# Causal masks of the second score pass: added by VectorE in PSUM instead of by a TensorE product, in a decoder trunk of two layers

## The reference

```python
def causal_block_attention(q, k, v, log_decay_cum=None):
    scale = q.shape[-1] ** -0.5
    for blk in range(T // Q_BLOCK):
        lo, hi = blk * Q_BLOCK, (blk + 1) * Q_BLOCK
        s = jnp.einsum('bqhd,bkhd->bhqk', q[:, lo:hi], k[:, :hi]) * scale
        ...
        mask = (lo + jnp.arange(Q_BLOCK))[:, None] >= jnp.arange(hi)[None, :]
        p = jax.nn.softmax(jnp.where(mask, s, -jnp.inf), axis=-1)
        outs.append(jnp.einsum('bhqk,bkhd->bqhd', p, v[:, :hi]))
```

## Time and profile before

| | |
|---|---|
| median of 3 runs | 2460.87 us (2460.1 to 2465.82) |
| span of the profiled execution | 2455.2 us |
| the six attentions together, in the span | 682.9 us |
| PE / DVE / ACT / POOL busy | 93% / 48% / 36% / 37% |

### The profile page before, as it was taken

The page is one execution under the profiler, slowest core; times in us unless marked ns, Lnnn a source line. Parts: engine busy times, 40 slices in busy tenths (PEclk is TensorE's granted clock), DMA queues, the critical chain, the costliest instruction groups (busy, mean ns, idle before and its releaser), DMA issues.

```text
span 2455.2 us, 35075 instructions
## 1 busy us (share of the span) xinstructions
PE 2293.2 (93%) x14164; PEld 1750.4 (71%) x14164; DVE 1172.6 (48%) x2262; ACT 876.3 (36%) x1444; POOL 902.2 (37%) x962
## 2 busy tenths in 40 slices
PE   7988999999999999879999889999999999998898
PEld 7866878986695876545697678789857859664456
DVE  4278243525336127666333881446162452277662
ACT  4332124714334334333333222156143244333341
POOL 2255112215525410555422642122345263115552
PEclk9989999999999999989999999999999999999899
DMA  4100232230100113100321003312301002131003
GB/s 151 56 19 1 87 107 87 70 137 1 35 18 1 50 56 120 60 1 1 138 70 56 19 2 98 121 61 95 112 1 35 18 1 69 37 137 43 1 1 129
DMA packets 92016, 141.28 MB, mean 58 GB/s; under 512 B 18352, under 2 KB 65488, under 8 KB 91856
## 3 DMA queue, kind: packets, MB, share of 16 engines
q1 hardware_dynamic: 91856, 139.05, 16.6%
HBM read 105.48 MB, written 33.55 MB: 57 GB/s over the span
## 4 chain that ended last, share of the span: by engine, by line
PE 79%; DVE 14%; ACT 2%; issue 2%; POOL 2%; DMA 0%; SPq 0%; POOLq 0%; DVEq 0%; ACTq 0%
PE psum L240 37%; PE psum L504 12%; PE psum L1392 5%; PE psum L1354 3%; DVE gla_A L766 3%; PE psum L1375 3%; PE psum L1340 3%; PE psum L1378 3%; PE psum L1380 3%; PE psum L745 2%; PE psum L1399 1%; PE psum L997 1%; POOL w_lo L198 1%; PE psum L1778 1%; PE psum L882 1%
## 5 line engine op out<-in xcount | busy, mean ns | idle before, releaser
L198 POOL TENSOR_TENSOR w_lo<-w_raw,w_hi 128x512 fp32r<-128x512 f32 (+3 forms) x240 | 322.1, 1374 | 823.6 <-ACT w_hi L189 823.6
L240 PE MATMUL psum<-h_hi,w_hi 128*128 128x512 f32 x768 | 200.8, 404 | 0.0
L240 PE MATMUL psum<-h_lo,w_hi 128*128 128x512 f32 x768 | 199.1, 403 | 0.0
L1587 POOL TENSOR_TENSOR mla_acc<-mla_acc,mla_p 128x512 f32<-128x512 f32 (+3 forms) x160 | 159.7, 1015 | 103.1 <-ACT mla_p L1446 103.1
L240 PE MATMUL psum<-h_hi,w_lo 128*128 128x512 f32 x768 | 192.2, 392 | 0.0
L240 PE MATMUL psum<-w_hi,h_hi 128*128 128x256 f32 (+3 forms) x1280 | 183.7, 286 | 0.0
L240 PE MATMUL psum<-w_hi,h_lo 128*128 128x256 f32 (+3 forms) x1280 | 179.6, 283 | 0.0
L240 PE MATMUL psum<-w_lo,h_hi 128*128 128x256 f32 (+3 forms) x1280 | 179.4, 283 | 0.0
L1587 POOL TENSOR_TENSOR fox_acc<-fox_acc,fox_p 128x512 f32<-128x512 f32 (+3 forms) x160 | 149.9, 958 | 75.5 <-ACT fox_p L1446 75.4
L189 ACT ACTIVATE w_hi<-w_raw 128x2048 fp32r<-128x2048 f32 (+3 forms) x60 | 113.6, 1893 | 175.1 <-PE psum L504 169.8
L240 PEld LDWEIGHTS psum<-h_lo,w_hi 128*128 128x128 f32 x768 | 147.7, 195 | 32.1
(11 more groups left out here) (324 smaller groups left out, 4428.8 us busy)
## 6 DMA issues: line engine op xcount, KB each, us to landing
w_raw<-in_w_in_dram SPq DMA_DIRECT2D x38, 1024.0 KB, 5.3
out_dram<-x_rows SPq DMA_DIRECT2D x64, 512.0 KB, 2.7
x_rows<-out_dram SPq DMA_DIRECT2D x56, 512.0 KB, 5.2
w_raw<-in_w_out_dram SPq DMA_DIRECT2D x16, 1024.0 KB, 6.5
x_first<-in_x_dram SPq DMA_DIRECT2D x8, 512.0 KB, 7.0
x_rows<-in_x_dram SPq DMA_DIRECT2D x8, 512.0 KB, 6.0
w_raw<-in_w_in_dram SPq DMA_DIRECT2D x2, 1088.0 KB, 8.7
w_raw<-in_w_in_dram SPq DMA_DIRECT2D x2, 1056.0 KB, 5.2
```

Source lines behind the costliest of these rows:

```text
L198: last = pool.tensor_tensor(self.w_lo[c["set"]][:, at], self.w_raw[c["set"]][:, at], self.w_hi[c["set"]][:, at].bitcast(F32), ALU.subtract)
L240: last = pe.matmul(o, lhs, rhs, start=(kk == 0 and n == 0), stop=(kk == KT - 1 and n == 2))
L1587: pool.tensor_tensor(acc, acc, p, ALU.add).then_inc(self.acc_done.sem, 1)
```

## The change

The product L1382 is gone. In its place VectorE adds a table `key_mask` (the mask with keys down the partitions, 128x128 in bf16) to the 128 queries in the bank, in place, after the third product of the unit (`mask`, waits for `st_done`). It is the first thing that VectorE does in unit j of `vector`. The exponents of diagonal units wait for that addition (`st_masked`) and no longer for TensorE. The identity in bf16, which only L1382 used, gives its place to the new table. The first pass is as it was.

```diff
@@ scores_turned
-        diagonal = kb >= 4 * c
-        last = pe.matmul(out, self.k_lo[ks][:, a, keys], self.q_hi[qs][:, a, lo:], start=False, stop=not diagonal)
-        if diagonal:
-            last = pe.matmul(k.psum[:, u % 2, lo:lo + P], k.mask_bf[:, :], k.ident_bf[:, :], start=False, stop=True)
-        last.then_inc(self.st_done.sem, 1)
+        pe.matmul(out, self.k_lo[ks][:, a, keys], self.q_hi[qs][:, a, lo:], start=False, stop=True)\
+          .then_inc(self.st_done.sem, 1)
@@ exponent
-        act.wait_ge(self.st_done.sem, self.st_done.at(u + 1))
+        if self.diagonal(i, j):
+            act.wait_ge(self.st_masked.sem, self.st_masked.at(self.masks(i, j) + 1))
+        else:
+            act.wait_ge(self.st_done.sem, self.st_done.at(u + 1))
@@ new
+    def mask(self, dve, i, j):
+
+        _, _, lo = self.unit(i, j)
+        u = self.t_base[i] + j
+        dve.wait_ge(self.st_done.sem, self.st_done.at(u + 1))
+        at = self.k.psum[:, u % 2, lo:lo + P]
+        dve.tensor_tensor(at, at, self.k.key_mask[:, :], ALU.add).then_inc(self.st_masked.sem, 1)
@@ vector
             for j in range(self.n_units(i)):
+                if self.diagonal(i, j):
+                    self.mask(dve, i, j)
                 if self.pre_at(i, j) is not None:
                     self.rest_of_group(dve, *self.pre_at(i, j))
                 for n in self.scores_at(i, j):
```

14 lines of the change are left out of this document (9 added, 5 removed).

## The result

The changed kernel takes 2544.74 us (median of 4 runs, 2533.53 to 2553.08) against 2462.67 us before (2460.1 to 2465.82): ratio 1.0339, 95% interval 1.0314 to 1.0364. Its profiled execution spans 2551.2 us, 96.0 more than the one before. The medians differ by 82.1 us only: the profiled execution of the change is the slowest of its four (2553.08 us), and that of before, at a span of 2455.2 us, is quick for its kernel. So some 14 of the 96.0 us come from which two executions were profiled.

The account below looks back on a forecast made before the run. TensorE was taken to dominate the last-ending chain (79%, VectorE 14%), with limits differing by item kind. 46 + 12 + 1.7 - 1.6 + 4.4 + 7 = 69.5 us on a 2460.9 us median gave 2530 us, range 2486 to 2558.

Parts of the forecast that it names:

- What goes: 256 TensorE products of L1382 removed, 0.04 to 0.05 us each; at most 12.8 us won, only where TensorE is the limit.
- What comes: 256 mask additions of 128x128 on VectorE: 0.20 us of its time each, 0.31 us from mask start to exponent's.
- Odd items: Ten items with a pair behind them: at units 8 to 12 ScalarE and VectorE alternate in one chain; 4.6 us each, 46 us.
- Even items: Ten items behind another: mask 5 stands behind `refine`, exponent 5 2 us late, `place_max` late; 1.2 us each, 12 us.
- First items: First items of the six attentions: most masks fall into VectorE's idle time, one of eight remains; 1.7 us in all.
- Last items: Last items of six attentions: fox 4 x -0.4 = -1.6 us; mla, mask 13 behind `outC.rest`, 2 x 2.2 = 4.4 us.
- The clock: TensorE, working in pieces in odd items, loses granted clock in half of the ten: 5 x 1.45 = 7 us.
- the rival that has it fall in all ten: TensorE's clock falls in all ten odd items and stays down longer: 29 instead of 7 us, 2552 us; chance 0.17.
- Outside the attentions: Everything outside the six attentions was expected to stay as before, with no term in the sum.
- that the back and forth costs much less: TensorE's product queue still sets the odd items' end, 1 us each; 27 us in all, 2488 us; chance 0.14.
- That the change is faster: VectorE, busy for 48%, takes masks in its gaps, exponents keep their places, TensorE gets 12.8 us: 2448 us; chance 0.05.

## Why the prediction was nearly right, step by step

The forecast was 2530 us, 2.8% slower, within 2486 to 2558; measured 2544.7. The direction, the mechanism and the place were right. By the profiled executions the growth is 96.0 us instead of 69.5: 4.5 less in waits (58 for 62.5), 11.8 more by the clock in the fox attentions (18.8 for 7), and 19.2 outside the attentions, for which the sum had nothing. Between the medians the growth is 82.1 us, 12.6 more than forecast. The forecast's own range, given as 2503 to 2556, is not what the bounds of its terms add up to, plainly summed (about 2505 to 2571).

- **What goes.** 0.05 us a product, 12.8 us: right; the items without any mask won 13.5.
- **What comes.** 0.31 us from the mask's start to the exponent's; it was 0.36 and 0.32 (1885.78 to 1886.14, 1155.37 to 1155.69). VectorE's next instruction stands 0.20 to 0.24 behind a mask. Right.
- **Odd items.** The steps were forecast as 3.18, 2.46, 2.59 and 2.66 us and came as 3.11, 2.44, 2.53 and 2.67; exponent 12 5.3 us late, measured 5.05; the item 4.6 us, measured 4.85 (fox item 1 of layer 1, mla item 5 of both layers). This is the step that carried the result, and it rested on following one unit around both engines in the order of the code. (The time of 1110.2 for the next item holds exponent 13's own 0.38 us as well, a term that the prediction doesn't name.) In mla items 1 to 3 the three together grew by 5.7 us instead of 10.4. That TensorE waits 8 us for the rotary product there, so that a late item 2 costs little, is in the trace of before and was not read. In those items the kernel before has a fallen clock of its own (at 0.50 for 27 us, 25 after), so waits and clock can't be parted exactly in the 5.7.
- **Even items.** 1.2 us each, measured 0.50 (0.77 in fox item 2 of layer 1). The chain was right, its first link too long: exponent 5 is 1.16 us late, not 2. Seen from the item's first exponent, `refine` began at 12.11 us instead of 12.79, since the maxima ahead of it came sooner, and VectorE's next instruction began 1.33 us later instead of 1.48. Of the 1.16 us the next item's first exponent keeps 0.50; TensorE makes up the rest.
- **First items.** 1.7 us in all, measured 6.6. In fox 0.30 to 0.38 each, as forecast. In mla 2.65: I had counted one mask, and missed that mask 7 stands behind the scaling of the keys, 3.6 us of VectorE. It is the same kind of place as `outC.rest` in the last item, which I did see.
- **Last items.** Fox 0.03 to 0.31 instead of -0.4, so the products gave nothing back there. mla 2.86 each instead of 2.2.
- **Luck in the waits.** That they came to 58 for 62.5 is partly luck. In each mla attention the items 1 to 3, 4 and 6 were priced 6.1 us too high (4.7 and 1.4), the items 0, 5 and 7 3.3 us too low (2.4, 0.3 and 0.6); in fox the sum is right to 0.3 us an attention.
- **The clock.** The term that was mis-sized most inside the attentions: 7 us, measured 18.8. I had half of ten items lose 1.45 us, from one stretch of the trace. It fell in three of four fox attentions, and then for 10 us and more at 0.50, also under the following even item: 4.4, 7.2 and 7.2 us. That it fell in three of four is nearer to the rival that has it fall in all ten, and its 2552 is 7 us above the median, where the forecast is 15 below. The Trainium skill (TensorE: Matmul & The Clock Gate, HAM oscillation — how this bites in real kernels) speaks for that rival; the trace agrees in part: the same stretch kept 1.00 in layer 1.
- **Outside the attentions.** "As before" was the expectation, and no instruction differs there. Yet the profiled execution lost 19.2 us: 3.2 and 3.0 between fox and mla, 8.5 between the layers, 4.2 behind the last exponent. The rows at 980 to 990 us above stand for these: clock at 0.65 and 0.67; in the same place of the kernel before it stood at 1.00:

```profile
955.00:960.00 5.00, 2.01 (x10) 1.00 0.00 1
```

  Every other kernel, the one without masks too, shows 5 to 16 us there against the same execution of before. So this one execution of before was a favourable one, or any shift of the attentions changes where the clock falls behind them. The runs speak for the first in part: a run's time is its span and about 1.9 us, so the profiled execution of before would be one of 2457.1 us, below each of its four timed runs (2460.1 to 2465.82), and outside the attentions the clock stood at 0.50 for 55 us in it, for 61 to 103 in all other kernels. How much is left for the second stays open.

The rivals: that the back and forth costs much less (2488) fell by the steps' lengths, which came as forecast to 0.07 us. That the change is faster (2448) fell likewise; its number is the time of no mask at all (2451), so as a bound it was right. The Trainium skill's rule to optimize the engine with the highest occupancy first (Perfetto Trace Analysis, Identifying the Most-Contended Engine) names the right engine here, since TensorE's relief alone was worth 8.6 us; what it doesn't price is the place where the work goes, and there the kernel lost 82. VectorE at 48% had the time, and time was not what the exponents waited for above all.

## What to carry to other kernels

A half idle engine doesn't take new work for nothing. Work that nobody waited for cost 23.5 us here; work that another engine waits for, behind an instruction that waits in its turn, cost 82. So ask what stands ahead of the new instruction, and not only how busy its engine is: follow one unit through both engines' orders, and if the new instruction closes a loop between them, its length is the sum of all links (2.5 us here, for a 0.3 us operation). If the work has to move, put it ahead of what waits for the other engine; that gave back 59 to 65 of 82 us here, but the same done where the new instruction itself waits for TensorE with maxima behind it made things worse by 29 us. And price beforehand what the move can win at all: here 8.6 us.

## What was not expected of the hardware

- A 128x128 addition on VectorE that reads PSUM (fp32) and a bf16 table in SBUF and writes PSUM took 283 to 333 ns, 300 in the median, also while GpSimd worked. One of the same shape that reads both tables from SBUF and writes bf16 to SBUF took 275 to 295 ns in 157 of 256 cases; in the other 99 it began during a GpSimd operation and ended 145 to 156 ns after the end of one, up to 1.40 us after its own start.
- Work on VectorE that nobody waits for still cost 23.5 us for 134.7 us of its time. In the items it is 24.0, 9.4 of it in the last ones, where all 48 operations were held so.
- The same instructions with the same busy TensorE (2.86 and 2.88 of 5 us) lost the clock in one layer (0.81, then 0.50) and kept it at 1.00 in the other. Four runs of the changed kernel differed by 19.5 us, in step with a mean clock of 0.957 to 0.968. The kernel before stayed within 5.7 us in four runs and within 11.4 us in thirteen (2456.47 to 2467.83, at 0.972 to 0.981).
